# Attention as one stream of head pairs, with values stationary in two column halves

## The chip, the cores and the metric

The kernel runs on one core of one Trainium2 chip. The metric is the device time of one execution in microseconds. Three runs of the kernel before gave 3447.33, 3456.71 and 3457.49 us; the median is 3456.71 us.

## The reference

One decoder layer on 1024 tokens of width 1024, in float32. Eight heads of width 64 use dilated windows (three patterns, merged by their softmax denominators), eight MLA heads use dense causal attention with queries and keys of width 96 (64 + 32 rotary) and values of width 64. What the sixteen heads give lies side by side in 1024 features, goes through an output product and is added to the residual. A PEER mixer with 16384 single-neuron experts and a last RMSNorm follow.

```
proj = rmsnorm(h, g_mix) @ w_in
o_a  = sum over patterns of softmax weight * dilated_window_attention(qa, ka, va)   # heads 0..7
o_m  = softmax(causal(q_m k_m^T * 96**-0.5)) @ v_m                                  # heads 8..15
h    = h + concat(o_a, o_m) @ w_out
h    = h + peer(rmsnorm(h, g_ffn));   return rmsnorm(h, g_final)
```

## The kernel before, in words

The stages run one after another, each as a block of five instruction streams (one for each engine and its queue) that starts when all engines have left the block before: `project_in`, `attend_pairs` (dilated heads), `attend` (MLA heads), `project_out`, then `route`, `spread_gates` and `run_experts`. At the start of a block `open_counts` and `clear_counts` let SyncE set the semaphores.

The merged dilated heads are one softmax per head: the mask holds minus the log of how many patterns reach a key, or 1e30. So both kinds of heads do the same work. A unit is one head and one tile of 128 queries. With tile i it has (i+1) blocks of 128 keys, since attention is causal. For one unit

- TensorE multiplies queries and keys into PSUM banks 0 to 3 (L881 for dilated heads, L653 for MLA heads);
- VectorE adds the mask, keeps the least value of each row and writes `sm` (L968, L742);
- ScalarE takes the exponential into `pr` and its row sums into `den` (L937, L711);
- TensorE turns `pr` in groups of up to four blocks into banks 4 and 5 (L892, L663), and ScalarE copies each group to `pT` (L924, L693);
- TensorE multiplies with the values: the turned probabilities of a block are the stationary operand, 128 columns, and the 64 columns of the values stream (L903, L672), so the sums leave with queries on partitions in banks 6 and 7;
- VectorE takes the reciprocal of `den` and scales the sum into `mix`, which has queries on partitions and features along the row (L974 and L976, L748 and L750).

`attend_pairs` takes two heads at a time. Their queries and keys, 64 features each, are turned together (L865), copied by ScalarE (L919), and the two heads' score products use the two row halves of the array. `attend` turns 96 features for each MLA head by itself (L642, L688); the rows from 96 on are filled with zeros by GpSimd (L697, L698), and TensorE waits for that at the start. Both run a `Fori` loop of four iterations with two heads each; every iteration begins with the turning of its queries and keys (`attend` turns the second head's at its place in the order) and ends with the last value product. The SyncE queue loads the next queries, keys and values from `scr_a` or `scr_m` once the old ones are used; the first ones are kept from `project_in`, which writes them by `first_heads` (L205 to L212). The load of `w_out` is issued at the start of `attend_pairs` (L828).

`project_out` works on tiles of 128 queries, two in turn. It turns a tile of `mix` by eight transposes (`turn_mix`, L1045), VectorE copies it to `mT` (`copy_mix`, L1121), and 16 float32 products with `w_out` follow (`multiply`, L1054), each of which the trace shows as two passes. VectorE adds the residual (L1127), the tile is normalised, turned again (L1062) and split. The first `copy_mix` stands behind VectorE's wait for `g_ffn`, which is loaded at the start of this block. On TensorE the order of a pair of tiles is multiply, `turn_hidden` of the tile before, `turn_mix` of the tile after next, multiply, and so on.

Of the kernel before, what the change touches and what calls it, by code (L numbers as in the profile page):

```python
# [6 lines left out]
P = 128  # L7
# [136 lines left out]
def project_in(core, heads_a, heads_m, mask, mask_in):  # L144
# [3 lines left out]
    with ExitStack() as ctx:  # L148
# [52 lines left out]
        def _(sp):  # L201
# [3 lines left out]
            def first_heads(dst, src, i, at, dim, sent):  # L205
                for t, a, w in zip(dst, at, (dim, dim, EA)):
                    if t.shape[1] == 2:
                        sp.dma_start(t[:, :, bass.ds(i, 1), :].rearrange("p k o w -> p k (o w)"),
                                     src[:, a:a + 2 * w].rearrange("p (k w) -> p k w", k=2)).then_inc(sent, 16)
                    else:  # L210
                        sp.dma_start(t[:, bass.ds(i, 1), :].rearrange("p o w -> p (o w)"), src[:, a:a + 2 * w]
                                     ).then_inc(sent, 16)  # L212
# [307 lines left out]
def attend(core, mix, mask, first, group, heads, dim, scr, q_at, k_at, v_at, mix_at,  # L520
           w_out=None, w_out_in=None):

    nc, ps = core.nc, core.ps
    ev = EA
    N = NT * 2
    with ExitStack() as ctx:  # L530
# [7 lines left out]
        g = lambda s: f"{s}_{group}"  # L538
        qn, kn, vn = first
        qT, kT = sb(g("qT"), [P, 2, SEQ]), sb(g("kT"), [P, 2, SEQ])  # L540
        sm = sb(g("sm"), [P, 2, SEQ])
        pr = sb(g("pr"), [P, 2, SEQ])
        pT = sb(g("pT"), [P, 2, NT, P])
        least = sb(g("least"), [P, N])
        den = sb(g("den"), [P, N])
        rden = sb(g("rden"), [P, N])
        qkv_in = [sem(g(f"qkv_in{k}")) for k in range(2)]
        qkv_used = [sem(g(f"qkv_used{k}")) for k in range(2)]
        score_done, masked_ready, prob_ready = sem(g("score_done")), sem(g("masked_ready")), sem(g("prob_ready"))
        turned = sem(g("turned"))  # L550
        out_act, out_dve = sem(g("out_act")), sem(g("out_dve"))
        pv_done, o_out = sem(g("pv_done")), sem(g("o_out"))
        q_rest, k_rest = sem(g("q_rest")), sem(g("k_rest"))
        dve_held, pe_held = sem(g("dve_held")), sem(g("pe_held"))
        scale = float(dim) ** -0.5


        fills, of_unit = [], {}
        order = []
        def fill(what):  # L560
            fills.append(what)
            return len(fills) - 1
        head_fills = {}

        def head_turn(k):
            head_fills[k] = [fill(("qk", k, z, half)) for z in range(2) for half in range(2)]
            order.append(("head", k))

        def score(u):
            if u < N:  # L570
                if u % NT == 0:
                    head_turn(u // NT)
                order.append(("score", u))

        score(0)
        score(1)
        for u in range(N):
            i = u % NT
            of_unit[u] = [fill(("p", u, b0, min(4, i + 1 - b0))) for b0 in range(0, i + 1, 4)]
            order.append(("turn", u))  # L580
            if u:
                order.append(("pv", u - 1))
            score(u + 2)
        order.append(("pv", N - 1))
        NFILL = len(fills)
        assert NFILL % 2 == 0

        def outs_before(n):

            return (n + 1) // 2, n // 2  # L590

        clear_counts(nc, made)
        open_counts(nc, (masked_ready, o_out, out_act, out_dve, prob_ready, pv_done, *qkv_in, *qkv_used, score_done,
                         turned))
        block = ctx.enter_context(nc.Block())

        @block.sync
        def _(sp):
            tiles = scr.rearrange("(i p) n -> p i n", p=P)
            for k in range(2):  # L600
                sp.sem_inc(qkv_in[k], 48)
            if w_out is not None:
                sp.dma_start(w_out[:, :, :], core.i["w_out"].rearrange("l (k p) n -> p (l k) n", p=P)
                             ).then_inc(w_out_in, 16)
            with sp.Fori(0, heads // 2 - 1) as it:
                for k in range(2):
                    sp.wait_ge(qkv_used[k], ONE + it + 1)
                    for dst, at, w in ((qn, q_at, dim), (kn, k_at, dim), (vn, v_at, ev)):
                        sp.dma_start(dst[:, k, :, :], tiles[:, :, bass.ds(it * (2 * w) + (at + 2 * w + k * w), w)]
                                     ).then_inc(qkv_in[k], 16)  # L610

        @block.tensor
        def _(pe):
            def wait_bank(it, n):

                a, d = outs_before(n)
                if n % 2 == 0:
                    pe.wait_ge(out_act, ONE + it * (NFILL // 2) + a)
                else:
                    pe.wait_ge(out_dve, ONE + it * (NFILL // 2) + d)  # L620

            def wait_copied(it, n):
                a, d = outs_before(n + 1)
                if n % 2 == 0:
                    pe.wait_ge(out_act, ONE + it * (NFILL // 2) + a)
                else:
                    pe.wait_ge(out_dve, ONE + it * (NFILL // 2) + d)

            pe.wait_ge(q_rest, 1)
            pe.wait_ge(k_rest, 1)  # L630
            with pe.Fori(0, heads // 2) as it:
                for kind, x in order:
                    if kind == "head":
                        pe.wait_ge(qkv_in[x], ONE + it * 48 + 48)
                        for n in head_fills[x]:
                            _, _, z, half = fills[n]
                            wait_bank(it, n)

                            pe.sem_inc(pe_held, 1)
                            src = (qn, kn)[z]  # L640
                            for j in range(4):
                                last = nc.tensor.transpose(ps[0:dim, 4 + n % 2, j * P:(j + 1) * P],  # L642
                                                           src[:, x, half * 4 + j, :], core.ident[:, :])
                            last.then_inc(turned, 1)
                        for n in head_fills[x][-2:]:
                            wait_copied(it, n)
                    elif kind == "score":
                        k, i, b = x // NT, x % NT, x % 2
                        nk = (i + 1) * P
                        pe.wait_ge(masked_ready, ONE + (it * N + x - 1 if x else it * N))  # L650
                        for c in range(0, nk, BANK):
# [14 lines left out]
                    else:  # L666
                        k, i, b = x // NT, x % NT, x % 2
                        for n in of_unit[x]:
                            wait_copied(it, n)
# [31 lines left out]
        def _(act):  # L701
# [12 lines left out]
            with act.Fori(0, heads // 2) as it:  # L714
                for kind, x in order:
                    if kind == "head":
                        for n in head_fills[x]:
                            copy_fill(act, it, n)
# [1709 lines left out]
```

## Time and profile before

| | us |
|---|---|
| median of three runs | 3456.71 |
| span of the profiled execution | 3450.1 |
| its dilated heads (291.7 to 496.5) | 204.8 |
| its MLA heads (496.5 to 706.6) | 210.1 |
| its output product (706.6 to 846.5) | 139.9 |

The stretch from 291.7 to 846.5 us is what the change touches, a sixth of the span. All else, mainly the experts from about 1520 us on, keeps its code. How to read the rows below: a line of a timeline merges equal instructions that follow one another on an engine, with their start, their length from the first start to the last end, and their number. PE is TensorE's products and PEld its loads of the stationary operand. A product's duration contains its way through the array, so that products that follow one another overlap by some 0.16 us. In a timeline a float32 product of values, scores or outputs counts as two passes, a transpose as one.

### The profile page before, as it was taken

To read this page: it belongs to the slowest core of one execution; us is meant where nothing else is said; L and a number is where in the kernel's file an instruction comes from. 1 tells how busy PE (TensorE), PEld (TensorE's weight loads), DVE (VectorE), ACT (ScalarE), POOL (GpSimd) and SP (SyncE) were. 2 spreads that over 40 slices of the span, in tenths; PEclk is the share of its full clock that TensorE was granted. 3 is DMA by queue.
4 is the path that set the end of the run, shared out by engine and by line. 5 is a ranking of instruction groups with operands and counts; after the bars stand their busy time and mean duration, and the time that the engine had idled before them with its cause. 6 is when DMAs were issued, how large, how long until landed. Compare 5 with 4: busy or idle time off the path is not lost.

```text
span 3450.1 us, 48239 instructions
## 1 busy us (share of the span) xinstructions
PE 3159.1 (92%) x17341; PEld 2491.1 (72%) x17341; DVE 2191.4 (64%) x5408; ACT 1062.5 (31%) x1512; POOL 981.2 (28%) x944
## 2 busy tenths in 40 slices
PE   8997889898899976679999999999999999999997
PEld 4445667654678866668888878887788888788885
DVE  2112333323888969968888777777777777544544
ACT  2224545511233238862222222222212222222221
POOL 0000000000122310003433356666556666222222
PEclk9998889999999989999999999999999999999998
DMA  5212101111111113698877789999999999675665
GB/s 194 84 65 104 35 6 37 36 57 58 58 48 67 50 38 104 190 300 288 283 270 259 248 339 378 359 371 379 339 368 378 378 356 372 255 259 214 246 229 199
DMA packets 319457, 715.66 MB, mean 207 GB/s; under 512 B 48672, under 2 KB 154400, under 8 KB 317856
## 3 DMA queue, kind: packets, MB, share of 16 engines
q0 software_dynamic: 110736, 403.23, 31.6%
q1 hardware_dynamic: 186128, 291.54, 23.9%
q10 hardware_dynamic: 22400, 18.37, 1.6%
q8 instruction: 115, 1.88, 0.2%
q14 instruction: 78, 0.64, 0.1%
HBM read 633.88 MB, written 75.50 MB: 206 GB/s over the span
## 4 chain that ended last, share of the span: by engine, by line
PE 51%; DVE 9%; DMA 1%; issue 1%; ACT 0%; POOL 0%; POOLq 0%; ACTq 0%; DVEq 0%; SPq 0%
PE psum L2050 24%; PE psum L2034 22%; PE psum L2077 5%; DVE first L1756 4%; DVE one L1749 1%; DVE second L1759 1%; DVE res L2226 1%; DVE res L2211 0%; DMA rows<-scr_rows 0%; DVE u_lo L2179 0%; DMA v_ring<-v_rows,eidT 0%; DVE w_lo L2196 0%; DVE v_lo L2201 0%; DMA scr_g<-gates 0%; POOL v_ring L2018 0%
## 5 line engine op out<-in xcount | busy, mean ns | idle before, releaser
L2018 POOL DMA_INDIRECT v_ring<-v_rows,eidT x384 | 444.0, 1156 | 625.5 <-PE psum L2077 516.9
L2034 PE MATMUL psum<-hn_hi_e,u_hi 128*128 128x320 f32 x1792 | 556.5, 311 | 10.3 <-PEq L103 5.2
L2034 PE MATMUL psum<-hn_lo_e,u_hi 128*128 128x320 f32 x1792 | 555.8, 310 | 0.0
L2034 PE MATMUL psum<-hn_hi_e,u_lo 128*128 128x320 f32 x1792 | 555.2, 310 | 0.0
L2050 PE MATMUL psum<-v_hi,w_hi 128*128 128x512 f32 x1280 | 512.0, 400 | 19.5 <-DVE coefT L2238 8.8
L2211 DVE TENSOR_TENSOR res<-psum,res 128x512 f32<-128x512 f32 x640 | 432.4, 686 | 127.8 <-PE psum L2050 127.4
L2050 PE MATMUL psum<-v_hi,w_lo 128*128 128x512 f32 x1280 | 501.3, 392 | 0.0
L2050 PE MATMUL psum<-v_lo,w_hi 128*128 128x512 f32 x1280 | 501.1, 392 | 0.0
L2011 POOL DMA_INDIRECT res<-u_rows,eid x288 | 332.2, 1154 | 295.0 <-DVE dots L2226 234.3
L2226 DVE CUSTOM_DVE_ANT_0 res<-res,rows 128x1024 f32<-128x1024 f32 x288 | 349.7, 1219 | 55.3 <-DMA res<-u_rows,eid 45.0
L2118 ACT ACTIVATE psum<-psum 128x640 f32<-128x640 f32 x112 | 77.1, 688 | 941.4 <-PE psum L2034 941.4
L2034 PEld LDWEIGHTS psum<-hn_hi_e,u_hi 128*128 128x128 f32 x1792 | 338.4, 189 | 15.6 <-issue 11.3
L2050 PEld LDWEIGHTS psum<-v_hi,w_hi 128*128 128x128 f32 x1280 | 241.3, 189 | 146.4 <-issue 80.1
L2034 PEld LDWEIGHTS psum<-hn_lo_e,u_hi 128*128 128x128 f32 x1792 | 338.2, 189 | 4.5
L2034 PEld LDWEIGHTS psum<-hn_hi_e,u_lo 128*128 128x128 f32 x1792 | 338.2, 189 | 0.0
L2191 DVE TENSOR_TENSOR w<-psum,w 128x640 f32<-128x640 f32 x112 | 92.3, 824 | 348.4 <-ACT psum L2118 333.4
L2050 PEld LDWEIGHTS psum<-v_hi,w_lo 128*128 128x128 f32 x1280 | 241.4, 189 | 51.6
L2050 PEld LDWEIGHTS psum<-v_lo,w_hi 128*128 128x128 f32 x1280 | 241.7, 189 | 46.6
L1774 PE MATMUL psum<-second,first 128*128 128x128 f32 x1280 | 163.7, 282 | 78.7 <-DVE second L1759 78.2
L2129 ACT ACTIVATE v_hi<-v_raw 128x1024 fp32r<-128x1024 f32 x128 | 128.4, 1051 | 328.0 <-PE psum L2050 328.0
L1774 PEld LDWEIGHTS psum<-second,first 128*128 128x128 f32 x1280 | 150.9, 194 | 91.6 <-DVE first L1756 91.6
L472 PE MATMUL psum<-w_in,hT 128*128 128x512 f32 (+1 forms) x512 | 211.0, 574 | 0.0
(248 smaller groups left out, 4664.1 us busy)
## 6 DMA issues: line engine op xcount, KB each, us to landing
v_raw<-v_rows SPq DMA_DIRECT2D x128, 512.0 KB, 6.8
u_raw<-uT SPq DMA_DIRECT2D x112, 512.0 KB, 6.4
w<-scr_g SPq DMA_DIRECT2D x128, 320.0 KB, 4.5
scr_g<-gates SPq DMA_DIRECT2D x4, 8192.0 KB, 30.6
scr_m<-st_m SPq DMA_DIRECT2D x8, 1024.0 KB, 4.1
w_raw<-in_w_pq SPq DMA_DIRECT2D x8, 1024.0 KB, 7.1
u_raw_r<-uT SPq DMA_DIRECT2D x16, 512.0 KB, 3.6
scr_g<-gates ACTq DMA_DIRECT2D x1, 7680.0 KB, 38.7
```

The lines of the kernel that those rows point to most:

```text
L472: last = nc.tensor.matmul(ps[:, 2 + c, 0:width(c)], hT[:, k, j, :], w_in[:, j, c * BANK:c * BANK + width(c)], start=j == 0, stop=j == KD - 1)
L1756: nc.vector.tensor_scalar(first[:, b, t, :], iota_f[:, :], flat[:, 0, at:at + 1], flat[:, 2, at:at + 1], ALU.is_equal, ALU.mult).then_inc( ...
L1774: last = nc.tensor.matmul(slot, first[:, b, t, :], second[:, b, t, :], start=True, stop=True)
L2011: pool.indirect_dma_start(u_slot(n % U_RING), None, core.i["u_rows"], bass.IndirectOffsetOnAxis(eid[:, n // P, n % P:n % P + 1], 0)).then_ ...
L2018: pool.indirect_dma_start(v_ring[:, m % V_RING, :], None, core.i["v_rows"], bass.IndirectOffsetOnAxis(eidT[:, m // P, t:t + 1], 0)).then_i ...
L2034: last = nc.tensor.matmul(ps[:, a, 0:COLS], x[:, c, j, :], y[:, j, a * COLS:(a + 1) * COLS], start=m == 0, stop=m == len(terms) - 1)
L2050: last = nc.tensor.matmul(ps[:, OUT_AT + F % OUT_BANKS, :], x[:, b, c, i * P:(i + 1) * P], y[:, c, half * BANK:(half + 1) * BANK], start=m ...
L2077: last = nc.tensor.matmul(ps[k * QUAD:(k + 1) * QUAD, SUM_AT + half, :], strip[:, p % 2, at:at + QUAD], v_ring[:, n % V_RING, half * BANK: ...
L2129: nc.scalar.activation(v_hi[:, c, :], v_raw[:, c, :], ACT.Copy).then_inc(v_hi_ready, 1)
L2191: nc.vector.tensor_tensor(half, ps[:, 0:ACTS, 0:COLS], half, ALU.mult).then_inc(w_ready, 1)
L2211: nc.vector.tensor_tensor(r, ps[:, OUT_AT + F % OUT_BANKS, :], r, ALU.add).then_inc(added, 1)
L2226: nc.vector.tensor_tensor_reduce(out=x, in0=x, in1=rows[:, :], scale=1.0, scalar=0.0, op0=ALU.mult, op1=ALU.add, accum_out=dots[:, tile % ...
```

## The change

`attend_pairs` and `attend` become one function, `attend`, with one unrolled stream of 64 steps: eight pairs of heads (four dilated, four MLA), each with eight tiles of queries. No loop and no block boundary is left between dilated and MLA heads, and `open_counts` goes from this block. In step s

- TensorE issues the scores of both heads of step s + 1, turns the probabilities of step s for both heads in turn (bank 4 for head 0, bank 5 for head 1), does the value product of step s - 1 (`weigh`) and turns what is due of the next pair's queries and keys (`turn_head`, one piece of four blocks in most steps: four pieces for a dilated pair, in steps 3 to 6 of the pair before, eight for an MLA pair, two in step 0 and one in each of steps 1 to 6);
- ScalarE copies the turned probabilities of head 0 and takes both exponentials of step s + 1; VectorE masks step s + 1 and copies those of head 1 (before, ScalarE copied all);
- in `weigh` the values are the stationary operand, 64 columns for each head, and the turned probabilities stream, 128 columns. Head 0 writes PSUM partitions 0 to 63, head 1 partitions 64 to 127 of one bank, so the sums leave with features on partitions;
- as the reciprocals now lie along the wrong axis, two more products with the reciprocals as stationary operand (one column repeated 64 times) and the identity streaming spread them over the partitions, ScalarE copies that to `rwide`, and VectorE multiplies sum and `rwide` into `mixT`, [features, queries], for both heads at once (`scaled`, in step s + 2).

`turn_head` waits (`o_out`) until `scaled` of two steps earlier has left the bank that it writes. GpSimd fills the zero rows of four of the eight turned query and key buffers at the start and of the other four when the dilated scores are done. `load_qk` and `load_v` replace the loads in the loops; `w_out` is loaded behind the first three of them. `project_out` uses `mixT` as the stationary operand as it lies: `turn_mix`, `copy_mix` and `mT` are gone. `first_heads` stores the two first MLA heads side by side, as for dilated heads.

The core of the diff:

```diff
-                        sp.dma_start(t[:, :, bass.ds(i, 1), :].rearrange("p k o w -> p k (o w)"),
-                                     src[:, a:a + 2 * w].rearrange("p (k w) -> p k w", k=2)).then_inc(sent, 16)
...
-def attend_pairs(core, mix, mask, first, group, heads, dim, scr, q_at, k_at, v_at, mix_at,
...
-            with pe.Fori(0, heads // 2) as it:
-                for kind, x in order:
...
-                            last = nc.tensor.matmul(ps[:, 6 + b, 0:ev], pT[:, b, j, :], vn[:, j, k * ev:(k + 1) * ev],
-                                                    start=j == 0, stop=j == i)
...
+def attend(core, mixT, mask, nat_a, nat_m, w_out, w_out_in):
...
+        def head_steps(p):
+            first = (3, 4, 5, 6) if in_a(p) else (0, 0, 1, 2, 3, 4, 5, 6)
+            return [(p - 1) * NT + i for i in first]
...
+            def load_qk(p):
+                need(sp, head_turned, pieces_before(p))
...
+            def load_v(p):
+                need(sp, pv_done, (p - 1) * NT if v_loads(p) > 1 or p == 2 or p == PAIRS - 2 else 0)
...
+            pool.memset(qk[EM:, 4:8, :], 0.0).then_inc(zero_high, 1)
+            pool.wait_ge(score_done, 2 * NT * PAIRS_A)
+            pool.memset(qk[EM:, 0:4, :], 0.0).then_inc(zero_low, 1)
...
+            def turn_head(p, n):
...
+                if p:
+                    need(pe, o_out, head_steps(p)[n] - 1)
+                    pe.wait_ge(head_copied, N)
...
+            def scores(s):
...
+                need(pe, masked_ready, 2 * s)
+                for c in range(0, nk, BANK):
+                    w = min(BANK, nk - c)
+                    for k in range(2):
+                        rows = slice(k * EA, (k + 1) * EA) if in_a(p) else slice(0, P)
+                        last = nc.tensor.matmul(ps[:, 2 * k + c // BANK, 0:w], qk[rows, slot(p, k, 0), i * P:(i + 1) * P],
+                                                qk[rows, slot(p, k, 1), c:c + w], start=True, stop=True)
...
+            def weigh(s):
...
+                need(pe, o_out, s - 1)
+                pe.wait_ge(head_copied, pieces_by(s))
+                for j in range(i + 1):
+                    for k in range(2):
+                        nc.tensor.matmul(ps[k * EA:(k + 1) * EA, bank, 0:P], v_of(p)[:, j, k * EA:(k + 1) * EA],
+                                         pT[:, s % 2, k, j, :], start=j == 0, stop=j == i)
+                pe.wait_ge(rden_ready, s + 1)
+                for k in range(2):
+                    last = nc.tensor.matmul(ps[k * EA:(k + 1) * EA, bank, P:2 * P],
+                                            rden[:, 2 * s + k:2 * s + k + 1].to_broadcast([P, EA]), core.ident[:, :],
+                                            start=True, stop=True)
+                last.then_inc(pv_done, 1)
...
+            for s in range(STEPS):
+                if s + 1 < STEPS:
+                    scores(s + 1)
+                for f in range(len(fills(s))):
+                    turn(s, 0, f)
+                    turn(s, 1, f)
+                if s:
+                    weigh(s - 1)
+                for p, n in due(s):
+                    turn_head(p, n)
...
+            for s in range(STEPS):
+                for f in range(len(fills(s))):
+                    copy_fill(act, copy, s, 0, f)
+                if s + 1 < STEPS:
+                    exp(s + 1, 0)
+                    exp(s + 1, 1)
+                if s:
+                    widen(s - 1)
+                for p, n in due(s):
+                    copy_head(p, n)
...
+            def scaled(s):
+                p, i, bank = s // NT, s % NT, OUT_BANK + s % 2
+                dve.wait_ge(wide_ready, s + 1)
+                nc.vector.tensor_tensor(mixT[:, p, i * P:(i + 1) * P], ps[:, bank, 0:P], rwide[:, s % 2, :], ALU.mult
+                                        ).then_inc(o_out, 1)
...
+            for s in range(STEPS):
+                if s + 1 < STEPS:
+                    masked(s + 1, 0)
+                copy_fill(dve, copy, s, 1, 0)
+                if s + 1 < STEPS:
+                    masked(s + 1, 1)
+                for f in range(1, len(fills(s))):
+                    copy_fill(dve, copy, s, 1, f)
+                inverse(s)
+                if s > 1:
+                    scaled(s - 2)
...
-                        last = nc.tensor.matmul(split_banks(k)[:, c, :], mT[:, k, j, :],
+                        last = nc.tensor.matmul(split_banks(k)[:, c, :],
+                                                mix[:, j, (n * 2 + k) * P:(n * 2 + k + 1) * P],
...
-            turn_mix(0, 0)
-            turn_mix(0, 1)
...
-            copy_mix(0, 0)
-            copy_mix(0, 1)
```

## Rows read from the trace of the kernel before

**Rows 1.** The page: busy time of TensorE; its granted clock in 40 slices.

```profile
PE 3159.1 (92%) x17341; PEld 2491.1 (72%) x17341; DVE 2191.4 (64%) x5408; ACT 1062.5 (31%) x1512; POOL 981.2 (28%) x944
...
PEclk9998889999999989999999999999999999999998
```

**Rows 2.** Windows by stage: length, busy time and count by engine, clock, DMA, GB/s.

```profile
291.70:496.50 204.80, 171.16 (x1120) 133.40 (x1120) 69.31 (x256) 104.38 (x244) 0.19 (x1) 0.87 0.14 44
496.50:706.60 210.10, 184.93 (x1184) 142.78 (x1184) 71.93 (x256) 113.67 (x256) 3.35 (x2) 0.96 0.14 30
706.60:846.50 139.90, 128.19 (x384) 64.88 (x384) 50.15 (x56) 19.83 (x33) 0.00 (x0) 0.94 0.10 35
```

**Rows 3.** The same by iteration: one of the dilated heads, one of the MLA heads.

```profile
342.00:392.50 50.50, 42.84 (x290) 33.92 (x290) 17.33 (x64) 25.99 (x61) 0.00 (x0) 0.90 0.11 31
...
602.00:653.00 51.00, 45.81 (x304) 35.60 (x304) 18.18 (x66) 28.27 (x64) 0.00 (x0) 1.00 0.19 41
```

**Rows 4.** Timeline, dilated heads, late tiles: start, length, engine, line, names, count, idle.

```profile
423.46 0.30 PEld L881 LDWEIGHTS psum<-kT_a,qT_a 64*128 64x128 f32 x4
423.46 1.77 PE L881 MATMUL psum<-kT_a,qT_a 64*128 64x512 f32 x8
...
425.17 0.88 PE L892 MATMUL psum<-ident,pr_a 128*128 128x128 f32 x6
425.43 1.09 DVE L968 CUSTOM_DVE_ANT_0 sm_a<-psum,mask 128x896 f32<-128x896 f32 x1 [1.39 <-PE psum L881]
...
426.44 1.08 DVE L968 CUSTOM_DVE_ANT_0 sm_a<-psum,mask 128x896 f32<-128x896 f32 x1
...
438.09 1.04 PE L892 MATMUL psum<-ident,pr_a 128*128 128x128 f32 x8
...
438.74 1.09 ACT L924 ACTIVATE pT_a<-psum 128x512 f32<-128x512 f32 x2 [0.65 <-PE psum L892]
...
438.97 3.68 PE L903 MATMUL psum<-vn_a,pT_a 128*128 128x64 f32 x32
```

**Rows 5.** Timeline of TensorE and VectorE at a seam of iterations and of stages.

```profile
391.75 1.06 PE L903 MATMUL psum<-vn_a,pT_a 128*128 128x64 f32 x8
...
397.07 0.49 PE L881 MATMUL psum<-kT_a,qT_a 64*128 64x128 f32 x4 [0.87 <-ACT kT_a L919]
...
493.67 0.28 DVE L976 TENSOR_SCALAR mix<-psum,rden_a 128x64 f32 x1 [1.44 <-PE psum L903]
...
504.91 1.62 PE L653 MATMUL psum<-kT_m,qT_m 128*128 128x128 f32 x4 [0.73 <-issue]
```

**Rows 6.** Timeline of TensorE, MLA heads, tile 5 of one head.

```profile
641.40 1.72 PE L653 MATMUL psum<-kT_m,qT_m 128*128 128x512 f32 x4
642.96 0.82 PE L663 MATMUL psum<-ident,pr_m 128*128 128x128 f32 x6
```

**Rows 7.** Groups by line and form, dilated heads: busy us, mean ns, idle before.

```profile
L903 PEld LDWEIGHTS psum<-vn_a,pT_a 128*128 128x128 f32 x576 | 75.2, 205 | 0.0
...
L968 DVE CUSTOM_DVE_ANT_0 sm_a<-psum,mask 128x128 f32<-128x128 f32 x8 | 2.3, 291 | 28.8 <-PE psum L881 28.6
```

**Rows 8.** The same over the span: loads of 128 and of 32 columns.

```profile
L2034 PEld LDWEIGHTS psum<-hn_hi_e,u_hi 128*128 128x128 f32 x1792 | 338.4, 189 | 15.6 <-issue 11.3
...
L2077 PEld LDWEIGHTS psum<-v_ring,strip 128*32 128x32 f32 x1536 | 40.4, 109 | 95.0 <-issue 95.0
```

**Rows 9.** Timeline of the output product's start.

```profile
711.24 1.23 DVE L1121 COPY mixT<-psum 128x1024 f32<-128x1024 f32 x1 [6.48 <-DMA g_ffn<-in_g_ffn]
...
714.29 15.02 PE L1054 MATMUL psum<-w_out,mixT 128*128 128x512 f32 x32
...
729.14 1.04 PE L1045 MATMUL psum<-ident,mix 128*128 128x128 f32 x8
...
730.01 13.90 PE L1054 MATMUL psum<-w_out,mixT 128*128 128x512 f32 x32
```

**Rows 10.** DMA issues: kind, count, KB each, median us to landing.

```profile
kn_m<-scr_m SPq DMA_DIRECT2D x6, 384.0 KB, 4.8
```

More of the change, by code:

```diff
@@ L549, in attend @@
[L549 to L583, printed above, removed]
@@ new lines, in v_of, with v_loads, slot, pieces @@
+        def v_of(p):
+            return (nat_a[2], v_more, nat_m[2])[v_place(p)]
+        def v_loads(p):
+            return sum(v_place(x) == v_place(p) and x not in (0, PAIRS_A) for x in range(p + 1))
+        def slot(p, k, z):
+            return p % 2 * 2 + z if in_a(p) else (1 - p % 2) * 4 + k * 2 + z
+        def pieces(p):
+            heads = (0,) if in_a(p) else (0, 1)
+            return [(k, z, half) for half in range(2) for k in heads for z in range(2)]
+        def pieces_before(p):
+            return sum(len(pieces(x)) for x in range(p))
@@ L597, in _, with fills_before, need, head_bank @@
+        def fills_before(s):
+            return sum(len(fills(x)) for x in range(s))
+        def need(eng, sem_, value):
+            if value > 0:
+                eng.wait_ge(sem_, value)
+        def head_bank(p, n):
+            return 4 + n if p == 0 else OUT_BANK + head_steps(p)[n] % 2
         @block.sync
         def _(sp):
[L599 to L610, printed above, removed]
+            tiles_a = core.scr_a.rearrange("(i p) n -> p i n", p=P)
+            tiles_m = core.scr_m.rearrange("(i p) n -> p i n", p=P)
@@ new lines, in _, with copy_fill @@
+            for n in range(len(pieces(0))):
+                turn_head(0, n)
+            scores(0)
+            for s in range(STEPS):
[8 more added lines that the diff above has]
+                    turn_head(p, n)
+            weigh(STEPS - 1)
+        def copy_fill(eng, copy, s, k, f):
+            b, nb = fills(s)[f]
+            eng.wait_ge(turned[k], fills_before(s) + f + 1)
+            if f == 0:
+                need(eng, pv_done, s - 1)
+            copy(pT[:, s % 2, k, b:b + nb, :], ps[:, 4 + k, 0:nb * P].rearrange("p (j t) -> p j t", t=P)
+                 ).then_inc(copied[k], 1)
@@ new lines, in _ @@
+            copy = lambda out, src: nc.scalar.activation(out, src, ACT.Copy)
+            for n in range(len(pieces(0))):
+                copy_head(0, n)
+            exp(0, 0)
+            exp(0, 1)
+            for s in range(STEPS):
[8 more added lines that the diff above has]
+                    copy_head(p, n)
```

498 lines of the change are left out of this document (132 added, 366 removed).

## The prediction

> **What bounds the kernel now.** I read the page first. TensorE is busy 92% of the span and its clock stands near full almost everywhere [rows 1], so the whole kernel is close to TensorE's pace and only the stages that the change touches need a closer look. The cut by stages is next: the eight dilated heads take 204.8 us, the eight MLA heads 210.1 us, the output product 139.9 us [rows 2]. In the first two, TensorE's busy time is 84% and 88%, and a busy TensorE includes overlapped pipeline tails, so I then cut them by loop iterations, 50.5 and 51.0 us each [rows 3]. Last comes the order of instructions inside an iteration [rows 4 to 6]: what is to be seen there is where TensorE pays and where it waits. It pays most in the value product. One key block of one head is two passes, each loading 128 stationary columns to stream only 64; 32 of them take 3.68 us, 0.11 us a pass [rows 4]. It waits at seams: from the last value product of a pair (391.75 + 1.06) to its next score at 397.07 are 4.3 us, and from the last write of the dilated stage to the first MLA score 11.2 us [rows 5].
>
> **Prices, all from rows at full clock.** n counts 128-column key blocks. A dilated pair's scores take 0.213 n + 0.21: 1.71 us to the next instruction at n = 7, with both heads' row halves at once [rows 4]. An MLA head takes 1.56 us at n = 6 [rows 6], of which 0.213 n is streaming, so two heads take 0.427 n + 0.28. The slope agrees with the output product: 32 passes of 512 columns in 13.90 us, 0.43 each, so 0.107 per 128 columns [rows 9]. The mask starts 0.26 after the scores' last issue (423.46 + 1.71 to 425.43) and holds VectorE 1.01 us at n = 7 (the next one starts then), 0.21 at n = 1 (0.29 busy less the 0.08 by which neighbours overlap): 0.07 + 0.134 n [rows 4, 7]. A VectorE copy out of PSUM has the same price (1.23 us for eight blocks [rows 9]). A transpose is 0.107, and its copier starts 0.22 after the last issue (438.09 to 438.74 for four) [rows 4].
>
> **The value product.** Before, one key block for two heads is 4 x 0.11 = 0.45 us. After, each pass loads 64 columns and streams 128, 0.107 us, and the heads write opposite column halves. No row shows column halves. The bounds are 2 x 0.107 = 0.21 (halves side by side, loads hidden) and 4 x 0.243 = 0.97 (nothing hidden: 0.136 us for a load of 64 columns, interpolated between 109 ns for 32 and 189 ns for 128 [rows 8], plus 0.107). I take 0.21, because the nearest row is that of the row halves: four score loads for two heads fit into 0.30 us and eight passes into 1.77, which only works two at a time [rows 4]. Over 8 pairs x 36 blocks = 288 blocks TensorE is spared 69 us, but much of it is under VectorE, as the steps show. Added beside it per step: four passes that spread the reciprocals (0.21 us), two changes of array layout (0.09 each, the shortfall in overlap at 425.17 [rows 4]), a 0.27 us ScalarE copy, an estimate from the mask's fixed part. ScalarE gives half of its transposed copies to VectorE; it has slack.
>
> **The steps.** One loop binds: scores of tile i+1 wait for both masks of tile i, and VectorE does mask, copy of head 1's first four blocks, mask, remaining copy, reciprocal, wide multiply in that order. Where a piece of the next pair's queries or keys is turned in the step, TensorE also waits for that wide multiply (o_out) before turning, and the next scores are queued behind it. So the step is one serial circle. Worked at i = 6 (n = 8 scored, 7 turned), dilated: scores 1.91, mask starts at 2.17, ends 3.32, copy to 3.92, mask to 5.06, copy of three to 5.54, reciprocal and multiply with their releases 0.43 to 5.97, turning 4 x 0.107 + 0.09 = 0.52: 6.49 us. MLA: scores 3.70, eight transposes and 0.22 to 4.77 (the mask ended earlier), copy to 5.38, mask to 6.52, copy to 6.99, then 0.43 and 0.52: 7.94 us. TensorE's own work there is 6.0 and 7.4 us. In the same way, i = 0 to 7 give 2.9, 2.5, 3.1, 4.7, 5.3, 5.9, 6.5, 4.5 = 35.3 us for a dilated pair and 5.3, 4.0, 4.9, 5.8, 6.6, 7.3, 7.9, 4.8 = 46.4 for an MLA pair (steps 0 and 7 are TensorE's, the rest this circle). The fourth pair turns eight MLA pieces, not four: 38.8. The last turns none: 40.3. Sum 3 x 35.3 + 38.8 + 3 x 46.4 + 40.3 = 324 us.
>
> Outside the steps: first pieces, scores and exponentials 5.5 us (from the seam's length and one score more), the last value product and its release 3 us. The clock is 0.87 in the dilated stage and 0.96 in the MLA stage now, but 1.00 by the iteration at 602 us [rows 2, 3], where TensorE works most densely. The new steps are about as dense; I charge 13 us of half-clock time, between 0 and 26 (a quarter of some 28 us of TensorE work per dilated pair, by the prices above, at double length would be 7 us each, half of it under VectorE). Both stages together: 346 + 2 us of exit (an estimate) = 348 against 414.9, so 67 us less.
>
> What hides the rest: loads of the next queries and keys are issued at a pair's step 6 and needed at the end of the next pair's step 0, some 8 us later; a 384 KB load takes 4.8 us to land [rows 10], two of 768 KB perhaps 8, so at worst 2 us in each of three pairs stand on the path. The output weights now queue behind the first three loads, far ahead of need. On GpSimd the two fills with zeros (now inside the 11.2 us seam) run beside dilated steps; the second is queued behind the last dilated score and waited for a whole pair later. Unrolling 64 steps removes loop ends; I cost its code at nothing, as the experts' unrolled code runs at TensorE's pace [rows 1]; at worst a few us.
>
> **Output product.** 64 transposes of the mixed rows and eight copies go. First product at 714.29 instead of right at the stage's start (706.6): 7.5 us, since the first copy stood behind the wait for g_ffn until 711.24. The six later turns are 0.87 us each (729.14 to 730.01) [rows 9]: 5 us. Together 12.5, all on TensorE's path. The DVE copies were covered by products and count nothing; what is late next is the product itself.
>
> **Sum.** 67 + 12.5 = 79.5 us off the span of 3450.1: 3370.6. The profiled span is 6.6 under the median of the runs, 3456.7 (its lowest run is 3447.3, so little lies around the span); the forecast is 3456.7 - 79.5 = 3377 us. Its own range, from the clock term (13 either way) and the loads and seams, is 3355 to 3400.
>
> **Rivals.** (1) The column halves take turns: 0.427 us a block. TensorE becomes the bound from step 3 on, and the steps sum to 374, 50 more: 3427. For it: no row shows two column halves at once. Against: the row halves.
> (2) The other side: loads are not hidden, in the value product alone. Load columns (0.83 ns each by [rows 8], 0.053 for 64) plus 0.107 is 0.16 a pass, 0.64 a block, and the steps sum to 429: 3377 + 105 = 3482; at 0.97 a block they sum to 522: 3575. It decides from about 0.54 a block, 0.135 a pass, where the steps reach 404 and the gain is used up. Against: full-array passes at 0.11 with loads of 205 ns [rows 4, 7] hide theirs.
> The Trainium skill, TensorE: Matmul & The Clock Gate, Part 3, section The mechanism, says that a load overlaps running matmuls only where the row group differs, and two column halves share all rows. By that rule a block would cost 0.32 us (halves side by side) to 0.64 (in turn), 3402 to 3482 us. The trace disagrees for the full array, since its loads too share all rows, and no run here shows it for column halves.
> (3) The steps run at half clock throughout the dilated pairs, as TensorE waits 0.5 to 1 us in most steps. Doubling TensorE's terms, a dilated pair comes to 57.7, 22.4 more, less some 10 already charged in all: 3377 + 80 = 3457. Against: it was 0.87 with longer waits.
>
> **How the numbers follow.** Forecast 0.67, halves in turn 0.18, loads exposed 0.09, half clock 0.06. The range reaches from 3350 to 3435: it holds the forecast and (1). A measurement of this kernel tells about 0.3%, 10 us, from no change. Faster: 0.67 + 0.18 + some of the others = 0.88; same 0.05; slower 0.07.
>
> **What would show it.** Right: the attention stretch near 346 us; a value product of 8 blocks for two heads near 1.7 us; VectorE's idle time ended by scores, TensorE's by masks and wide multiplies; no transposes ahead of the output product. Wrong: that group at 3.4 us (1) or over 5 (2); a clock near 0.5 in the dilated steps (3); TensorE waiting for head loads or for code.

## The result and the profile after

The changed kernel takes 3361.8 us (median of four runs, 3358.06 to 3365.18), the kernel before 3455.9 us (median of four, 3447.33 to 3457.49). The ratio is 0.9732 with a 95% interval of 0.9719 to 0.9746: 94 us or 2.7% less. The forecast was 3377 us, with a range of 3350 to 3435.

The page of the changed kernel first: busy time of TensorE and its granted clock in 40 slices, which answer to [rows 1].

```profile
PE 3103.4 (92%) x17533; PEld 2420.4 (72%) x17533; DVE 2200.9 (65%) x5368; ACT 1032.4 (31%) x1477; POOL 988.1 (29%) x944
...
PEclk9998999998999899999999999999999999999998
```

TensorE's share is 92% as before. The page tells nothing more of the change, since the stretch in question is a sixth of the span. The windows by pair of heads, which answer to [rows 2, 3], tell it (start and end, length, busy time and count of PE, PEld, DVE, ACT and POOL, then granted clock, DMA share, GB/s). They are, in order, pair 0 with the start, the second dilated pair, the fourth, the first MLA pair, the last pair with the exit, and the output product.

```profile
292.90:335.60 42.70, 38.53 (x298) 26.06 (x298) 20.02 (x62) 26.23 (x63) 3.51 (x1) 0.86 0.48 160
335.60:372.10 36.50, 33.34 (x314) 22.83 (x312) 19.83 (x60) 22.24 (x56) 0.00 (x0) 1.00 0.16 45
...
408.70:448.60 39.90, 35.57 (x331) 24.39 (x329) 19.82 (x60) 24.52 (x60) 3.51 (x1) 1.00 0.09 25
448.60:493.70 45.10, 40.74 (x331) 28.72 (x329) 20.05 (x60) 24.44 (x60) 0.00 (x0) 1.00 0.17 48
...
583.90:628.00 44.10, 39.43 (x330) 27.15 (x328) 20.12 (x58) 19.62 (x50) 0.00 (x0) 1.00 0.01 1
628.00:757.40 129.40, 119.90 (x320) 56.64 (x320) 40.94 (x48) 19.83 (x33) 0.00 (x0) 0.95 0.11 38
```

A dilated pair takes 36.6 us where an iteration took 50.5, an MLA pair 45.1 where it took 51.0 [rows 3]. The clock is 1.00 in every pair but the first. From its first product to the first product of the next stage, attention fell from 414.7 us (292.05 to 706.79) to 335.1 (293.0 to 628.1): 79.6 us less. From there to the first `minus_ident` on ScalarE, the mark that both kernels share at the start of `route` (848.26 before, 757.49 after), the output product fell from 141.5 to 129.4 us: 12.1 less. In these two executions the stages around them differ by 5 us the other way (1 ahead of the stretch, 4 behind it), and the spans by 86.7; the two kernels' own runs scatter over 10 and 7 us.

The timeline of TensorE, all of step 5 of an MLA pair, and the start of the output product, which answers to [rows 9] (start, length, engine, line, names, count, and in brackets idle time and what ended it):

```profile
473.90 3.17 PE L670 MATMUL psum<-qk_turned 128*128 128x512 f32 x8
476.91 1.04 PE L681 MATMUL psum<-ident,pr 128*128 128x128 f32 x8
478.19 0.97 PE L681 MATMUL psum<-ident,pr 128*128 128x128 f32 x4 [0.25 <-ACT pT L751]
479.10 1.31 PE L696 MATMUL psum<-pT,vn_m 128*64 128x128 f32 x20
480.24 0.39 PE L700 MATMUL psum<-ident,rden 128*64 128x128 f32 x4
480.56 0.64 PE L650 MATMUL psum<-ident,qn_m 128*96 128x128 f32 x4
481.04 3.60 PE L670 MATMUL psum<-qk_turned 128*128 128x512 f32 x8
...
628.12 17.38 PE L871 MATMUL psum<-w_out,mix_turned 128*128 128x512 f32 x36 [2.12 <-PEq L94]
```

Scores (L670), turning (L681), values (L696), the spreading of the reciprocals (L700) and a piece of the next pair (L650) follow one another. In 7.14 us the rows show one wait, 0.25 for ScalarE's copy. A second one, for VectorE's copy, lies inside the row of four turns, which takes 0.97 us where the row of eight takes 1.04. The value product of five blocks for two heads is 1.31 us; one of three blocks is 0.88 (below), so one block costs 0.215. Before, eight blocks of one head took 3.68 [rows 4]. The output product begins at the start of its stage, with nothing turned ahead of it.

The loads of the values, grouped by form (busy time, mean ns of one, idle before):

```profile
L696 PEld LDWEIGHTS psum<-pT,v_more 128*64 128x64 f32 x576 | 30.8, 136 | 5.0 <-issue 3.4 <-ACT pT L751 1.2
```

TensorE's waits in the attention stretch, behind its first product (total us, times, longest):

```profile
PE psum L650 <- issue: 9.3, 12, 0.8
PE psum L681 <- ACT pT L751: 7.8, 31, 0.3
PE psum L670 <- DVE least L775: 5.2, 10, 0.7
PE psum L650 <- ACT qk_turned L735: 3.1, 4, 0.8
PE psum L650 <- DVE mix_turned L787: 2.1, 3, 0.8
PE psum L681 <- DVE pT L725: 1.6, 8, 0.2
```

A load of 64 columns takes 136 ns, and yet a block with four of them costs 215 ns: the loads are hidden. All waits that the profile counts are 29 us of 335 together, in short pieces; none is put down to a head's load. They cost more than is counted: turns of one row start every 0.11 us but last 0.27 each, so the first 0.16 us in which nothing new starts do not show as idle. What the row "issue" is shows in step 3 of a dilated pair, all engines:

```profile
381.03 1.35 PE L670 MATMUL psum<-qk_turned 64*128 64x512 f32 x8 [0.54 <-DVE least L775]
...
383.33 0.88 PE L696 MATMUL psum<-pT,vn_a 128*64 128x128 f32 x12
...
384.04 0.39 PE L700 MATMUL psum<-ident,rden 128*64 128x128 f32 x4
384.05 0.82 DVE L775 CUSTOM_DVE_ANT_0 sm<-psum,mask 128x640 f32<-128x640 f32 x1
...
...
384.87 0.27 DVE L787 TENSOR_TENSOR mix_turned<-psum,rden_turned 128x128 f32<-128x128 f32 x1
385.24 0.63 PE L650 MATMUL psum<-ident,qn_a 128*128 128x128 f32 x4 [0.81 <-issue]
385.79 0.70 PE L670 MATMUL psum<-qk_turned 64*128 64x512 f32 x2
```

TensorE is through with the spreading at 384.43 and then stands for 0.81 us, until VectorE has masked, inverted and multiplied (L787, ended 385.14), as `turn_head` may write its bank only then. The profile put three such waits down to VectorE and twelve to "issue". They are 15, one in each of the steps 1 to 3 that turn a piece, and 11.4 us in all.

### The profile page after: what moved, and what is told of

The parts are those of the page before. It is cut to its first block, busy times and chain, and to the rows that moved or that the text cites. A ratio compares the mean times of both kernels' runs of the same rounds, so it can differ in the third digit from the quotient of the medians.

```text
span 3363.4 us, 47386 instructions
## 1 busy us (share of the span) xinstructions
PE 3103.4 (92%) x17533; PEld 2420.4 (72%) x17533; DVE 2200.9 (65%) x5368; ACT 1032.4 (31%) x1477; POOL 988.1 (29%) x944
## 4 chain that ended last, share of the span: by engine, by line
PE 53%; DVE 9%; DMA 1%; issue 1%; ACT 0%; POOL 0%; POOLq 0%; ACTq 0%; DVEq 0%; SPq 0%
PE psum L1850 25%; PE psum L1834 23%; PE psum L1877 5%; DVE first L1556 5%; DVE one L1549 1%; DVE second L1559 1%; DVE res L2026 1%; DVE res L2011 0%; DMA rows<-scr_rows 0%; DVE u_lo L1979 0%; DMA v_ring<-v_rows,eidT 0%; DVE w_lo L1996 0%; DVE v_lo L2001 0%; DMA scr_g<-gates 0%; POOL v_ring L1818 0%
## 5 line engine op out<-in xcount | busy, mean ns | idle before, releaser
L2026 DVE CUSTOM_DVE_ANT_0 res<-res,rows 128x1024 f32<-128x1024 f32 x288 | 350.5, 1222 | 56.0 <-DMA res<-u_rows,eid 45.1
L1834 PEld LDWEIGHTS psum<-hn_hi_e,u_hi 128*128 128x128 f32 x1792 | 338.9, 189 | 15.7 <-issue 11.4
```

The costliest lines, as they stand in the source:

```text
L1834: last = nc.tensor.matmul(ps[:, a, 0:COLS], x[:, c, j, :], y[:, j, a * COLS:(a + 1) * COLS], start=m == 0, stop=m == len(terms) - 1)
L2026: nc.vector.tensor_tensor_reduce(out=x, in0=x, in1=rows[:, :], scale=1.0, scalar=0.0, op0=ALU.mult, op1=ALU.add, accum_out=dots[:, tile % ...
```

## The experiments

Times are medians of four runs each. The first four were timed against 3455.7 us, the last three against 3453.2. The lengths of the steps, from the start of one step's scores to the next, carry most of the argument; the first two lines are the working of the prediction and what the changed kernel showed (a dash: not used):

| us, steps 0 to 7 | dilated pair | MLA pair |
|---|---|---|
| forecast | 2.9 2.5 3.1 4.7 5.3 5.9 6.5 4.5 | 5.3 4.0 4.9 5.8 6.6 7.3 7.9 4.8 |
| changed kernel | 3.12 2.50 3.28 4.76 5.47 5.99 6.65 4.79 | 5.26 3.64 4.56 5.48 6.39 7.14 7.89 4.75 |
| heads in turn | 4.48 2.49 3.28 4.77 5.94 6.70 7.58 5.92 | 6.63 3.64 4.55 5.48 6.88 7.84 8.81 5.89 |
| scaling first | - - - 3.91 5.45 6.00 6.65 4.78 | - 2.89 3.98 4.80 6.48 7.14 7.89 4.75 |
| reciprocal of 128 | - - - 5.51 6.05 6.53 7.13 - | - 4.39 5.30 6.23 6.98 7.67 8.36 - |
| head's piece between | - - - - 4.91 5.45 6.11 - | - - - - 5.95 6.60 7.37 - |

**Do the column halves run side by side?** The same products with the two loops exchanged: all blocks of head 0, then all of head 1.

```diff
-                for j in range(i + 1):
-                    for k in range(2):
+                for k in range(2):
+                    for j in range(i + 1):
```

> The value product issues all blocks of head 0 and then all of head 1, instead of alternating; same products, same column halves. If two halves run side by side only when their passes are issued alternately, a block for two heads costs 0.43 us instead of 0.22. By the prediction's circle through VectorE part of this is covered: the steps sum to 374 instead of 324, about 3412 us. If TensorE's own work sets every step, nothing is covered: 288 x 0.213 = 61 us more, about 3423. If the array pairs halves whatever the order, or the halves never mattered: about 3362.

Measured: 3395.5 us (3394.51 to 3399.93), ratio 0.9833 (0.9816 to 0.9849), 33.7 over the changed kernel. Two steps of an MLA pair, TensorE's timeline:

```profile
488.69 1.25 PE L696 MATMUL psum<-pT,vn_m 128*64 128x128 f32 x13
489.68 0.32 PE L700 MATMUL psum<-ident,rden 128*64 128x128 f32 x1
...
496.09 1.69 PE L696 MATMUL psum<-pT,vn_m 128*64 128x128 f32 x17
497.52 0.32 PE L700 MATMUL psum<-ident,rden 128*64 128x128 f32 x1
497.62 0.27 PE L696 MATMUL psum<-pT,vn_m 128*64 128x128 f32 x1
```

Four passes more take 0.44 us more, 0.11 a pass: these have no partner. The loads stay hidden even so. The whole price would be 288 blocks x 0.22 = 63 us, and about half of it came, because the halves do not take turns in full. By the single starts in the trace, which the rows merge, the last four passes of head 0 and the first four of head 1 start in turn, 0.05 us apart, in every tile of three blocks or more; in tiles of one and two blocks, with two and four passes a head, all run side by side as before. The rows show the same at the end: a spreading pass of head 0 (L700 at 497.52) starts ahead of value passes of head 1 that stand before it in the program (L696 at 497.62 and after). So the halves run side by side where their instructions stand within about four passes of each other, and the order between them is not kept.

From its first start to its last, the value product grew by 0, 0.01, 0.27, 0.49, 0.70, 0.92, 1.14 and 1.36 us for one to eight blocks. Step 0, which does the eight blocks of the tile before, and steps 4 to 7 grew by just that. In step 3 the 0.27 us went into the wait for VectorE, as the step kept its length.

**Which steps does VectorE bind?** The scaling of two steps earlier is put at the start of VectorE's step, ahead of both masks, instead of at its end.

```diff
             for s in range(STEPS):
+                if s > 1:
+                    scaled(s - 2)
                 if s + 1 < STEPS:
                     masked(s + 1, 0)
...
                 inverse(s)
-                if s > 1:
-                    scaled(s - 2)
```

> VectorE does the wide multiply of step s-2 at the start of step s, while it waits for scores anyway, and not at the end. By the circle of the prediction the turning of heads no longer waits for VectorE's whole step: the steps sum to 310.5 instead of 324, about 3348 us. If TensorE's own work sets the steps, only the few waits that end with the wide multiply go (2 to 5 us): 3357 to 3360.

Measured: 3349.8 us (3349.01 to 3353.43), ratio 0.9700 (0.9683 to 0.9716), 12.0 less than the changed kernel. The same step 3 of a dilated pair:

```profile
380.03 1.35 PE L670 MATMUL psum<-qk_turned 64*128 64x512 f32 x8 [0.54 <-DVE least L775]
...
383.04 0.39 PE L700 MATMUL psum<-ident,rden 128*64 128x128 f32 x4
383.36 0.66 PE L650 MATMUL psum<-ident,qn_a 128*128 128x128 f32 x4
383.94 1.56 PE L670 MATMUL psum<-qk_turned 64*128 64x512 f32 x8
```

The 0.81 us ahead of L650 is gone and the step falls from 4.76 to 3.91. The gain is in the 15 waits counted above (11.4 us), of which this run's trace shows none; steps 4 to 7 keep their length, but for step 4 of an MLA pair, which grew by 0.09. So the wait for the scaling held steps 1 to 3 alone, and from step 4 on TensorE sets the pace, with its own work and its waits for copies of turned groups. The time alone would have misled: it lies by the 3348 us expected of the circle, only because the few waits of the other account were 11.4 us and not 2 to 5.

**Stream or value product?** The stream of 64 steps as it is, with the value product, the layout of `mix` and the `project_out` of before: no halves, no spreading.

```diff
-                        nc.tensor.matmul(ps[k * EA:(k + 1) * EA, bank, 0:P], v_of(p)[:, j, k * EA:(k + 1) * EA],
-                                         pT[:, s % 2, k, j, :], start=j == 0, stop=j == i)
+                        last = nc.tensor.matmul(ps[:, bank, k * EA:(k + 1) * EA], pT[:, s % 2, k, j, :],
+                                                v_of(p)[:, j, k * EA:(k + 1) * EA], start=j == 0, stop=j == i)
```

> The stream of 64 steps as it is, but the value product as in the kernel before: turned probabilities stationary, 64 columns of values stream, sums scaled per head into mix with queries on partitions, no spreading of reciprocals, and the output product turns its tiles again as before. A block costs 0.45 instead of 0.22 us (288 blocks, 66 us), the spreading of 0.39 us a step goes (25 us), the output product gives back 12. TensorE's own work: +41 +12, about 3415 us. The circle: +45 +12, about 3419. If the stream alone made the gain: about 3375; if the column halves alone made it: about 3455.

Measured: 3413.0 us (3411.46 to 3413.71), ratio 0.9878 (0.9861 to 0.9894). One of its windows in the dilated heads, columns as above:

```profile
335.00:375.00 40.00, 36.76 (x273) 28.74 (x271) 21.31 (x68) 20.55 (x48) 0.00 (x0) 1.00 0.14 40
```

The stream alone is worth 42.7 us (with VectorE's half of the copies, which no run takes out of it), the new value product with its output product 51.2 more, of which the output product is some 12. From 335 us on the stream is at full clock with the old product too, where the loop of before had 0.90 [rows 3]. So the clock was given back by the stream, not by the new product.

**Is the spreading worth making cheaper?** The reciprocal writes every value 64 times, and one transpose spreads it instead of two products.

```diff
-                for k in range(2):
-                    last = nc.tensor.matmul(ps[k * EA:(k + 1) * EA, bank, P:2 * P],
-                                            rden[:, 2 * s + k:2 * s + k + 1].to_broadcast([P, EA]), core.ident[:, :],
-                                            start=True, stop=True)
+                last = nc.tensor.transpose(ps[:, bank, P:2 * P], rden[:, s % 2, :], core.ident[:, :])
...
-                nc.vector.reciprocal(rden[:, 2 * s:2 * s + 2], den[:, 2 * s:2 * s + 2]).then_inc(rden_ready, 1)
+                nc.vector.reciprocal(rden[:, s % 2, :].rearrange("p (k e) -> p k e", e=EA),
+                                     den[:, 2 * s:2 * s + 2].rearrange("p (k o) -> p k o", o=1).to_broadcast([P, 2, EA])
```

> VectorE writes each reciprocal 64 times in a row (128 instead of 2 elements, about 0.13 us more a step), and TensorE spreads them by one transpose of 128 columns (one pass) instead of four passes in column halves. The spreading falls from 0.32 to about 0.11 us of TensorE. If TensorE's own work sets the steps: 64 x 0.2 = 13 us less, about 3349. By the circle only steps 0 and 7 of a pair gain and the longer VectorE step costs: 3358 to 3366.

Measured: 3388.6 us (3386.94 to 3391.02), ratio 0.9811 (0.9794 to 0.9827), 26.8 slower than the changed kernel: a miss. Groups on VectorE, first this kernel, then the changed kernel:

```profile
L780 DVE RECIPROCAL rden<-den 128x128 f32<-128x128 f32 x64 | 60.5, 945 | 0.0
```

```profile
L782 DVE RECIPROCAL rden<-den 128x2 f32<-128x2 f32 x64 | 10.1, 158 | 0.0
```

A reciprocal of 128 elements takes 0.945 us, one of two 0.158: 0.79 more, where the mask's price for 128 columns had led to expect far less. It stands in VectorE's circle and lengthens the steps that turn a piece, by 0.75 in step 3 (steps 1 to 3 of an MLA pair) and by 0.47 to 0.60 in steps 4 to 6. In these, then, VectorE had only some 0.2 to 0.3 us to spare, a near tie. The next run keeps the transpose and shortens the reciprocal.

**The spreading in one pass, without the long reciprocal.** The scaling first, as above, then a reciprocal of two values, a copy that repeats them 64 times, and one transpose.

```diff
-                nc.vector.reciprocal(rden[:, 2 * s:2 * s + 2], den[:, 2 * s:2 * s + 2]).then_inc(rden_ready, 1)
+                nc.vector.reciprocal(rden[:, 2 * s:2 * s + 2], den[:, 2 * s:2 * s + 2]).then_inc(inv_ready, 1)
+                nc.vector.tensor_copy(rspread[:, s % 2, :].rearrange("p (k e) -> p k e", e=EA),
+                                      rden[:, 2 * s:2 * s + 2].rearrange("p (k o) -> p k o", o=1).to_broadcast([P, 2, EA])
```

> As e2_scaled_first, and the spreading of reciprocals is one transpose of 128 columns as in e4_rden_turned; but the reciprocal stays at two elements (0.16 us) and a copy of 128 elements writes them 64 times in a row. If e4 lost its 27 us to the 0.95 us reciprocal inside VectorE's chain and not to the transpose, this one must gain where TensorE's own work sets the step (0, 4 to 7): about 0.2 us in 40 steps, 8 us, 3341 to 3344. If the transpose is what cost: 3365 or more.

Measured: 3350.4 us (3348.41 to 3352.43), ratio 0.9702 (0.9685 to 0.9718): no difference from scaling first alone. The copy's group:

```profile
L783 DVE COPY rden_spread<-rden 128x128 f32<-128x128 f32 x64 | 14.6, 227 | 6.5
```

The copy costs 0.23 us where the long reciprocal cost 0.79 more, and the loss is gone with the transpose kept, so the transpose was not its cause. That leaves the long reciprocal, in the order where VectorE's step still ended with the scaling; with the scaling first it was not run. Steps 4 to 6 gained only 0.11 us each (5.35, 5.89 and 6.54 in a dilated pair), and the expected gain is not seen in the median.

**The waits between the groups.** In steps 4 to 6 the profile counts 0.25 us of waiting for ScalarE's copy of the first turned group and up to 0.2 more for VectorE's, the more the smaller the second group. The piece of the next pair is turned in between.

```diff
                 for f in range(len(fills(s))):
                     turn(s, 0, f)
                     turn(s, 1, f)
+                    if f == 0:
+                        for p, n in due(s)[:1]:
+                            turn_head(p, n)
                 if s:
                     weigh(s - 1)
-                for p, n in due(s):
+                for p, n in due(s)[1:]:
```

> As e5_one_pass_spread, and the piece of the next pair's queries or keys is turned between the first and the second group of probabilities (the first piece of a step; the second one stays at the end), where TensorE waits 0.25 us for ScalarE's copy and some 0.1 for VectorE's. It applies in steps 4 to 6 of seven pairs: 21 x 0.3 = 6 us under e5 if TensorE's own work sets these steps. If VectorE's chain sets them: no change.

Measured: 3338.9 us (3337.03 to 3342.39), ratio 0.9667 (0.9651 to 0.9683), 11.5 less than the kernel without this edit. An MLA step 6:

```profile
466.01 3.60 PE L671 MATMUL psum<-qk_turned 128*128 128x512 f32 x8
469.44 1.04 PE L682 MATMUL psum<-ident,pr 128*128 128x128 f32 x8
470.32 0.60 PE L651 MATMUL psum<-ident,kn_m 128*96 128x128 f32 x4
470.75 1.06 PE L682 MATMUL psum<-ident,pr 128*128 128x128 f32 x6
471.74 1.53 PE L697 MATMUL psum<-pT,vn_m 128*64 128x128 f32 x24
473.21 0.33 PE L700 MATMUL psum<-ident,rden_spread 128*128 128x128 f32 x1
473.37 0.61 PE L671 MATMUL psum<-qk_turned 128*128 128x128 f32 x4
```

The step takes 7.36 us, where it took 7.79 without this edit and 7.89 in the changed kernel. The wait for ScalarE's copy is gone, as the piece runs in it. The one for VectorE's copy is still there, inside the row of six turns, and the sums of these waits in the profile are as before (1.6 us, 8 times). Steps 4 to 6 each gained 0.42 to 0.44 us, from a wait counted as 0.25: by the starts in the trace, the turn behind it came 0.52 us after the one before it, where turns follow at 0.11, so it cost 0.41. That makes about 9 us of the 11.5; the rest is within the scatter of the runs. This is the fastest version tried, 23 us under the changed kernel and 3.3% under the one before.

**What do the seams cost?** The changed kernel with all pieces of the next pair in step 6 instead of spread over the steps.

```diff
-            first = (3, 4, 5, 6) if in_a(p) else (0, 0, 1, 2, 3, 4, 5, 6)
+            first = (6,) * len(pieces(p))
```

> The changed kernel, but all pieces of the next pair are turned in step 6, one after the other with the copy between, as at a seam of the kernel before; order, products and copies are the same. By the terms of the prediction steps 1 to 5 get shorter and step 6 longer by 1.29 us a piece: the steps sum to 344 instead of 324, about 3382 us, with the clock at full. If such a seam also drops TensorE to half clock (the term of 13 us that was charged), the steps behind it run double: some 5 us for each of seven pairs more, about 3415, with a granted clock well under 1.00 behind each step 6.

Measured: 3404.3 us (3401.58 to 3404.94), ratio 0.9853 (0.9837 to 0.9870), 42.5 slower than the changed kernel. Windows ahead of, in and behind the seam of one MLA pair:

```profile
495.00:501.00 6.00, 5.75 (x51) 3.90 (x49) 3.79 (x8) 3.13 (x5) 0.00 (x0) 1.00 0.00 0
501.00:507.00 6.00, 2.67 (x18) 1.56 (x16) 0.00 (x0) 2.82 (x8) 0.00 (x0) 1.00 0.00 0
507.00:512.00 5.00, 2.90 (x12) 2.07 (x13) 0.00 (x0) 1.59 (x3) 0.00 (x0) 0.53 0.00 0
```

TensorE's timeline in the seam of the next pair:

```profile
557.46 0.61 PE L650 MATMUL psum<-ident,kn_m 128*96 128x128 f32 x4 [0.77 <-ACT qk_turned L735]
558.85 1.06 PE L650 MATMUL psum<-ident,qn_m 128*96 128x128 f32 x4 [0.77 <-ACT qk_turned L735]
```

In the seam TensorE turns a piece (0.61), waits for ScalarE's copy of it (0.77), turns the next: busy 2.67 us of 6. Behind that the clock falls to 0.53, the level of 1.2 GHz, and the same four turns take 1.06. An MLA step with a seam takes 19.0 to 19.5 us. At full clock it would take 17.8, an estimate from TensorE's timeline: 7.5 to the first piece, seven times 1.39 to the last, 0.56 to the next scores. Step 7 behind it takes up to 6.75 instead of 4.75. Summed over the steps of the two traces the seams cost 40 us: in the same way some 27 are the waits, where 20 were expected, and some 13 the low clock, where 33 were. Not every seam brings it: the third (409 to 414 us) has the same four pieces and the same waits of 0.78 as the second, but the clock stayed at 1.00 behind it, where it was 0.72 behind the second (374 to 380 us).

## Why the prediction was right, and where it was off

**The value product: right.** Halves side by side with hidden loads gave 0.215 us a block, against 0.21 taken. Rival (1) falls by this. The run with heads in turn is a milder case of it, since four passes of each half still overlap; it cost 34 us, and the rival's 50 was not put to the test. Rival (2) falls by the loads of 136 ns that nobody waits for. The rule of the Trainium skill that stood behind it (TensorE: Matmul & The Clock Gate, Part 3, The mechanism) is that only different row groups let a load overlap running products. By the prediction's estimate it would have cost at least 0.32 us a block; the trace disagrees for column halves, which share all rows, as it did for the full array.

**The sum of the steps: right, its reason half wrong.** 325.7 us against 324, in part by luck: a dilated pair took 36.6 us against 35.3, an MLA pair 45.1 against 46.4, and the two errors cancel. The claim was that one serial circle over VectorE binds steps 1 to 6. Scaling first took the wait for the scaling away and only steps 1 to 3 gained, 12 us; from step 4 on TensorE was itself the bound. It cost little because the two are near ties there: at step 6 the circle was put at 6.49 and 7.94 us, TensorE's own work at 6.0 and 7.4, and TensorE's side came out at 6.65 and 7.89. The 0.65 and 0.49 us that were missing are covered, by the starts in the trace, by the two waits for copies between turned groups, which the prediction did not name: 0.41 for ScalarE's, which the run with the piece between took out again, and 0.26 (dilated) and 0.15 (MLA) for VectorE's.

**The clock: the term that was mis-sized.** 13 us were charged for half-clock time in the dilated steps, the middle between 0 and 26, and about 1 was paid, in pair 0 (37.6 us of steps where the second has 36.6; it was more than 1 by itself, since the first step of pair 0 has no value product to do). The reason given beside the charge was right and pointed to none: the new steps are "about as dense" as the iteration at 602 us, which ran at 1.00, and TensorE's busy share is 0.91 and 0.90 in a dilated and an MLA pair, where it was 0.90. What the prediction lacked is where the low clock of before lay. The kernel before, behind the seam at 393 us, columns as above:

```profile
392.50:397.00 4.50, 2.49 (x19) 1.86 (x18) 0.28 (x1) 2.17 (x4) 0.00 (x0) 1.00 0.41 117
...
400.00:406.00 6.00, 5.12 (x21) 3.52 (x20) 2.91 (x15) 2.74 (x10) 0.00 (x0) 0.50 0.39 95
...
410.00:443.00 33.00, 28.67 (x222) 23.88 (x221) 12.84 (x44) 18.95 (x40) 0.00 (x0) 1.00 0.00 0
```

It lay in the first tiles behind a seam; the later and longer ones, with the same products, ran at 1.00. The stream with the old product ran at 1.00 too, and putting seams back brought 0.53. Rival (3), half clock in all dilated steps, falls by the 1.00 of every pair but the first: waits of 0.5 to 0.8 us in single steps leave the clock there. These 12 us are nearly the whole difference between the attention stretch forecast (348) and measured (335.1).

**The rest.** The output product gave 12.1 against 12.5. Loads, zero fills and 64 unrolled steps, costed at nothing or nearly so, cost nothing that a wait shows. The start took 5.0 us against 5.5, the end and exit 4.4 against 5. The stages around, costed at no change, were 5 us longer in the profiled execution (4 of them behind the stretch); whether by chance or by what the change left in the queues is not settled, as the executions of one kernel scatter by as much. One row was read from the wrong end: from the end of the last dilated write (493.67 + 0.28) to the first MLA score are 11.0 us, not 11.2; no term rests on it.

**What stays open.** What it takes for the clock to fall: one seam in the run with the pieces in step 6 kept 1.00, as did an MLA iteration of the kernel before [rows 3]. The double piece in step 0 of an MLA pair (5.26 us, where the last pair without pieces took 3.39) was not tried elsewhere. And the wait for VectorE's copy of the first turned group is still in the fastest version.

## What to carry to other kernels

When two candidates for the bound come close in a step (6.49 and 6.0 us here, before two waits were added), write both sums with all their terms: neither a step length forecast rightly nor the time of a run shows which engine sets it, only an edit to one of them and the lengths of the steps do. Price a wait from start to start: here 0.25 us of counted idle time cost 0.41. A seam between iterations costs its waits and, behind most of them, a low clock, so spread the next iteration's preparation over the steps, and put it where TensorE waits for a copy. For small matrices in two column halves, alternate the instructions of the halves: of two long runs, one behind the other, only the four passes on either side of the change overlap.

## What the hardware showed that was not expected

- Two 64-column halves of the array run side by side with alternating instructions (0.215 us for four passes of 128 columns), at 0.11 a pass without (0.44 for the four), with their loads of 136 ns hidden in both cases. With all of one half ahead of the other, four passes of each still overlap at the change, and a pass of one half can start ahead of passes of the other that stand before it in the program.
- A reciprocal on VectorE takes 0.158 us for two elements a row and 0.945 for 128, some 6 ns for each further element; a copy of 128 takes 0.227.
- TensorE busy 2.67 us of 6 in pieces of 0.61 was followed by a granted clock of 0.53, while steps with single waits of 0.5 to 0.8 us kept 1.00, and so did one seam of four pieces with waits of 0.78.
